# Expert blocks of 168 slots instead of 192, and gathers that leave out padded slots, in a fused decoder-layer kernel

## The reference, cut to what matters

```python
scores = jax.nn.sigmoid((x @ lp['router_w']).astype(jnp.float32))
_, idx = lax.top_k(scores + lp['router_bias'].astype(jnp.float32), TOP_K)      # 8 of 64 experts
gate = jnp.take_along_axis(scores, idx, axis=-1)
gate = gate / jnp.sum(gate, axis=-1, keepdims=True) * ROUTED_SCALE
...
def swiglu(x, w_gate, w_up, w_down):
    return (jax.nn.silu(x @ w_gate) * (x @ w_up)) @ w_down
...
routed = jax.ops.segment_sum(y, tok, num_segments=N)      # y: each expert's rows, times gate
return routed + swiglu(x, lp['w_sh_gate'], lp['w_sh_up'], lp['w_sh_down'])
```

## Time and profile before

| | |
|---|---|
| median of three runs | 2907.5 us |
| profiled execution, device time | 2899.51 us |
| its span, first to last instruction | 2896.6 us |
| mean granted TensorE clock in it | 0.954 |
| first `gate` matmul of the first expert block (L1955) | at 1755.67 us |
| first `gate` matmul of the last, 64th, block | at 2813.67 us |
| PE busy, of the span | 2581.3 us (89%) |
| DVE busy | 1356.9 us (47%) |
| ACT busy | 1054.3 us (36%) |
| POOL busy | 595.0 us (21%) |

### The profile page before, as it was taken

How to read it: one execution, slowest core, us unless ns; L and a number is a source line. 1 busy time by engine, 2 the same in 40 slices (tenths; PEclk the granted TensorE clock), 3 DMA queues, 4 the chain that set the end, 5 groups by cost and what they waited for, 6 DMA issues and landing times. The chain is left out here.

```text
span 2896.6 us, 38101 instructions
## 1 busy us (share of the span) xinstructions
PE 2581.3 (89%) x13546; PEld 1943.9 (67%) x13546; DVE 1356.9 (47%) x2762; ACT 1054.3 (36%) x1687; POOL 595.0 (21%) x421
## 2 busy tenths in 40 slices
PE   7879997989996659999999697999999999999990
PEld 5447775656445555666645346898998898998990
DVE  0423334520007640100146425777777777777774
ACT  1133333320002210000012005666666676766762
POOL 1010002200000000000004402344343443443433
PEclk9989998999999979999999798999999999999995
DMA  4000003321001014111013118999999999999974
GB/s 123 0 15 0 0 0 148 146 84 37 0 0 40 0 35 130 29 37 43 0 57 100 45 73 288 273 292 277 284 290 281 283 287 274 289 283 286 283 192 149
DMA packets 151712, 395.12 MB, mean 136 GB/s; under 512 B 43318, under 2 KB 87430, under 8 KB 125014
## 3 DMA queue, kind: packets, MB, share of 16 engines
q1 hardware_dynamic: 116166, 269.90, 27.7%
q0 software_dynamic: 35488, 124.43, 17.7%
HBM read 325.74 MB, written 69.13 MB: 136 GB/s over the span
## 5 line engine op out<-in xcount | busy, mean ns | idle before, releaser
L1958 PE MATMUL banks<-split 128*128 128x384 f32 x1792 | 538.6, 363 | 0.0
L2072 DVE TENSOR_TENSOR split<-rest,split 128x2048 fp32r<-128x2048 f32 x192 | 438.8, 2285 | 108.7 <-ACT split L2016 108.7
L1956 PE MATMUL banks<-split 128*128 128x192 f32 x2048 | 482.9, 256 | 0.0
L1978 PE MATMUL banks<-split 128*128 128x512 f32 x1536 | 406.5, 407 | 22.9 <-ACT rest L2029 18.8
L1956 PEld LDWEIGHTS banks<-split 128*128 128x128 f32 x2048 | 389.3, 192 | 2.7
L2016 ACT CAST split<-rest 128x2048 fp32r<-128x2048 f32 x192 | 359.3, 1904 | 66.0 <-DMA rest<-in_w_exp_gate 61.0
L1408 PE MATMUL banks<-big 128*128 128x368 f32 x1152 | 358.6, 474 | 15.2 <-DMA big<-in_w_br_hg 15.2
L1906 POOL DMA_INDIRECT y_rows<-rest x128 | 271.3, 2119 | 335.3 <-ACT rest L2029 298.5
L1958 PEld LDWEIGHTS banks<-split 128*128 128x128 f32 x1792 | 339.1, 189 | 0.0
L1978 PEld LDWEIGHTS banks<-split 128*128 128x128 f32 x1536 | 276.4, 190 | 78.3 <-ACT rest L2029 23.0
L1408 PEld LDWEIGHTS banks<-big 128*128 128x128 f32 x1152 | 219.9, 191 | 153.5 <-issue 17.3
(11 more groups left out here) (331 smaller groups left out, 3343.6 us busy)
## 6 DMA issues: line engine op xcount, KB each, us to landing
rest<-in_w_exp_gate SPq DMA_DIRECT2D x64, 1024.0 KB, 9.7
rest<-in_w_exp_up SPq DMA_DIRECT2D x64, 1024.0 KB, 6.0
rest<-in_w_exp_down SPq DMA_DIRECT2D x64, 1024.0 KB, 7.2
big<-in_w_in SPq DMA_DIRECT2D x27, 512.0 KB, 4.1
big<-in_x_prompt SPq DMA_DIRECT2D x14, 512.0 KB, 5.9
x_rows<-big SPq DMA_DIRECT2D x9, 512.0 KB
y_rows<-big SPq DMA_DIRECT2D x9, 512.0 KB, 2.6
big<-in_w_in SPq DMA_DIRECT2D x1, 4096.0 KB, 15.4
```

What stands on the lines that cost most here:

```text
L1956: ins = pe.matmul(PS[:, banks[f], 0:CAP], wr[:, s, j, LO, at:at + 128], x[:, k, 0:2], start=False, stop=False)
L1958: ins = pe.matmul(PS[:, banks[f], 0:2 * CAP], wr[:, s, j, HI, at:at + 128], x[:, k], start=False, stop=(k == KD - 1))
L1978: ins = pe.matmul(PS[:, DBANK[c]], hr[:, a, f, HALF * hf:HALF * hf + 128], wr[:, s, DOWN, b, at:at + 512], start=(f == 0 and j == 0), stop ...
L2072: dve.tensor_tensor(wr[:, s, j, LO], raw[:, s, j], wr[:, s, j, HI].bitcast(F32), ALU.subtract).then_inc(parted[j], 1)
```

## The change

CAP goes from 192 to 168, and with it every size that is made from it: HALF from 96 to 84, VCAP from 1152 (6 * 192) to 1176 (7 * 168), KOVER from 5 to 6, the table's slots from 73920 to 75432. The rows behind T are written no more and `x1_rows` ends at T. The gathers are given `bounds_check=T - 1, oob_is_err=False`: an entry whose row number is over T - 1 is to be left out, and the row of the buffer stays as it is. So that nothing undefined stands there at first, POOL fills the gather buffer with zeros once, ahead of its first gather, and waits for that.

```diff
-CAP = 192
+CAP = 168
 HALF = CAP // 2
 VCAP = -(-T // CAP) * CAP
...
-        sp.dma_start(S.x1_dram[T:T + 128], S.x1[:, 0]).then_inc(x1_out, 16)
-        sp.dma_start(S.x1_dram[T + 128:T + CAP], S.x1[0:CAP - 128, 1]).then_inc(x1_out, 16)
-        sp.wait_ge(x1_out, 16 * (NT + 2))
+        sp.wait_ge(x1_out, 16 * NT)
...
-    passed = sem("e_passed")
+    passed, xg_zero = sem("e_passed"), sem("e_xz")
...
                 pool.indirect_dma_start(out=xg[0:HALF, s, hf], out_offset=None, in_=S.x1_dram,
-                                        in_offset=bass.IndirectOffsetOnAxis(ap=gi[0:HALF, s, 2 * hf:2 * hf + 1].bitcast(I32), axis=0)
-                                        ).then_inc(xg_in[s], 16)
+                                        in_offset=bass.IndirectOffsetOnAxis(ap=gi[0:HALF, s, 2 * hf:2 * hf + 1].bitcast(I32), axis=0),
+                                        bounds_check=T - 1, oob_is_err=False).then_inc(xg_in[s], 16)
...
         for s in range(2):
             pool.sem_inc(si_free[s], 1)
+        pool.memset(xg.rearrange("p a b c -> p (a b c)")[0:HALF], 0.0).then_inc(xg_zero, 1)
+        pool.wait_ge(xg_zero, 1)
         gather(0, 0)
         gather(1, 0)
...
-        S.x1_dram = nc.dram_tensor("x1_rows", [T + CAP, DM], F32).ap()
+        S.x1_dram = nc.dram_tensor("x1_rows", [T, DM], F32).ap()
```

## The result

| | before | after |
|---|---|---|
| median of 11 runs each, same chip | 2911.65 us | 2921.63 us |
| lowest to highest | 2904.23 to 2917.02 | 2911.84 to 2930.65 |
| ratio, with 95% interval | | 1.0035 [1.0021, 1.0049] |
| profiled execution, its own time | 2899.51 us | 2921.63 us |
| its span | 2896.6 us | 2919.4 us |

The forecast was 2897 us and faster; the measured time is inside the range, on the other side of no change. The two profiled executions differ by more (22.8 us of span) than the medians do (10.0 us), because the stages ahead of the expert blocks also took longer in the second: the expert stage's first instruction is at 1740.47 us in the trace of before and at 1750.89 us in that of after. So I compare the expert stage alone, from there to the first instruction of the next stage (2842.05 and 2865.36 us): 1101.6 us before, 1114.5 after, +12.9 us.

The account below looks back on a forecast made before the run. PE was taken to bound the expert blocks, with DMA nearly full. The loop's 15.8 us plus 0.15 for the late entries gave 15.95 per block: -9.5 us, last block -0.8, together -10.3, so 2897 us; range 2874 to 2926.

Parts of the forecast that it names:

- Two more blocks: Expert blocks: 66 instead of 64, each a full one; at 16.62 us each that alone is +33.2 us.
- PE's floor: PE's own work per expert block: from 16.21 to 15.40 us, through shorter wide matmuls and transposes.
- DMA relief: DMA engines in the expert blocks: 82 rows less per block at 287 ns a row, 1.5 us of 15.8 less.
- The loop: From one odd block's scatter through the next gather to the next odd scatter: 32.70 us to 31.6 per two blocks.
- The sign that was named: In the expert blocks, PE's transposes would wait for the gather in every second block.
- The late entries: ACT's wait for table entries requested behind the `down` matrix: 0.15 us per block left of the 0.41 excess.
- Ends: First and last expert block: 3.5 us fill and first period 1.3 us shorter, together nothing; last block 0.8 us shorter.
- The slower rival: Expert blocks: the loop does not shrink and gathers get dearer, 16.4 us per block, +19 us, 2926 us; chance 0.21.
- threshold of 32.4 us: Length of the loop over which, in the slower rival, 66 blocks cost more than 64 did.

Follow-up runs that it names:

- cap_168: The kernel before with blocks of 168 slots in place of 192, gathers without a bounds check; ratio to before 1.0066.
- skip_192: The kernel after with blocks of 192 slots in place of 168, padded rows still left out of gathers; ratio to before 0.9975.
- ent_168: The kernel after with the table entries requested ahead of the `down` matrix; ratio to before 0.9938.
- gat_168: The kernel after with the next even block's gather issued ahead of the wait for the odd block's scatter to land; ratio to before 0.9927.
- skip_184: The kernel after with blocks of 184 slots in place of 168, so halves of 92 rows; ratio to before 1.1446.
- both_168: The kernel after with table entries requested ahead of `down` and the gather ahead of the wait for the scatter; ratio to before 0.9844.
- both_192: The kernel before with table entries requested ahead of `down` and the gather ahead of the wait for the scatter; ratio to before 0.9918.
- gat_192: The kernel before with the next even block's gather issued ahead of the wait for the odd block's scatter; ratio to before 0.9959.

## Why the prediction failed

- **Two more blocks.** Right: 66, all of full length.
- **PE's floor.** Right: forecast 15.40 us, measured 15.35. The narrow matmul stayed at 0.11 us. The wide one lost the 0.02 us that the forecast gave it (0.179 to 0.156 us, medians). The Trainium skill's rule in "TensorE: Matmul & The Clock Gate", section LDWEIGHTS, is columns / 1.2 ns, an estimate of 107 ns for 128 columns, and the row of the narrow one agrees with it.
- **DMA relief.** The rows were as counted, their price not. q0 took 16 x 800 x 0.371 = 4749 us for 14,976 rows, 317 ns each where the earlier trace rows gave 287. Per block that is 96.6 us of engine time in place of 109.9: 0.8 us of relief on each of 16 engines, not 1.5. The small packets are little of it, 92 us in all (56 before). A packet of 4 KB itself took 311 ns on average where it took 284 before; it took 300 in cap_168 and in skip_192. Why is open.
- **The loop.** Right: forecast 31.6 us for two blocks, one is 31.41 in the trace. Forecast for the loop as the only wait: 15.8 us per block; ent_168, which has that wait alone, takes 15.72, so 31.44 for two. The sign that was named, a wait of the transposes for the gather in every second block, came in part: 17 times in 32 pairs. There is luck in the size: the forecast was the middle of two bounds, and the relief that it leaned on was half of what it assumed.
- **"The late entries remain, but a block that they stretch gives the next gather time, so the two don't add up: of the 0.41 us I leave 0.15."** This is the step that failed. The loop alone cost 0.37 us (ent_168), near the 0.40 of the forecast, and both waits 0.93 (after), so that the entries on top of the loop were 0.56 where 0.15 was left for them. Alone they cost 0.60 in the trace of gat_168, and some 0.37 by the median of its runs. Two errors lie in the step. I took the cost of the entries at its old size. Their way hardly changed: ACT's first part in even blocks begins 12.64 us after the block's start before (median) and 12.70 after. But in blocks without a wait it began at 12.20 us before and at 11.40 after: the deadline came 0.8 us nearer with PE's floor, and the waits went from 57.0 us in 19 to 72.1 us in 20. The same thing that I had worked out for the loop, a fixed way against a shorter block, I did not work out for the entries. And I argued, without a row, that a block which the entries stretch would give the gather time. It gives little: odd blocks, which hold the gather's wait, take 15.90 us after and 16.02 in ent_168, 0.06 us per block on average, while even ones take 16.66 after and 15.42 in ent_168. With 0.56 in the place of 0.15 and the measured floor and loop the sum is 15.35 + 0.37 + 0.56 = 16.28 us, 64 x 16.28 = 1042 against 1030, the +11.4 us of the trace; since 0.56 is itself the difference of after and ent_168, this locates the miss and doesn't test it.
- **Ends.** The fill took 3.51 us as forecast, and the first gather came 4.56 us after the stage's first instruction in place of 3.22. The first period is 0.7 us longer where I had it 1.3 shorter, and its rate fell from 364 to 351 GB/s. Little can be read from that: over all runs the first period was 24.2 to 30.5 us, one execution each. The last block, which I had 0.8 us shorter, was 0.4 longer, from its first matmul to the next stage.
- **The slower rival.** Its sum, 16.4 us per block, came near to 16.28, with half of its reason. The packet counts fit 84 rows on 14 engines, and the gather's instruction on POOL takes 1042 ns (median) where it took 943; half of that is the bounds check, for in cap_168 it takes 992. But the loop did shrink, and both waits are as large in cap_168, which has no bounds check. What it priced by the loop alone is for the larger part the entries. And its threshold of 32.4 us was too high: 64 blocks of 16.10 us already take the 1030.3 us of before, so that with 0.15 for the entries a loop of over 31.9 us was enough for slower. The forecast of 31.6 was 0.3 us away from it.

Of the 12.9 us that the stage became longer, 11.4 are the middle periods, 0.7 the first one, 0.4 the stretch ahead of it and 0.4 the last block. The part ahead of the stage, 10.4 us, is in code that the change doesn't touch but for two writes less in routing and a longer slot table. Medians put the whole difference at 10.0 us.

## What to carry to other kernels

When an edit makes the bounding engine faster, list every transfer that lands close to its deadline, and move each deadline by the gain. A latency that cost 0.17 us per block at a block of 16.2 us cost 0.60 at 15.4 in the traces (0.24 and 0.37 by the medians). Before shrinking a tile, look at what is issued ahead of the small transfers (1.5 KB behind 1 MB here) and at what a gather is queued behind: two reorderings without any less work gave 0.8% here, and 1.6% together with the smaller tile that alone had cost 0.66%. And choose row counts of indirect transfers so that 16 divides them, or test them at the size meant: 92 rows cost 6.6 us per block with the old orders, 84 rows nothing with the new ones.

## What the runs showed of the hardware

- **The row count of an indirect transfer matters, not only its size.** By the packet counts the rows on the fullest engine are 6, 6, 5, 8 and 23 for 96, 84, 80, 88 and 92 rows. 92 rows made a block 6.6 us longer than 96 did, with the DMA engines busy 0.67 of the time.
- **A long wait costs clock too.** PE's granted clock was 0.86 in the middle periods of skip_184, in which PE was idle for 363 of 1429 us; the others have 0.98 to 1.00. In the middle periods of both_168, with no idle time, it never left the upper level; in after 17.1 of 1041.7 us were at the lower.
- **A left-out row is a packet all the same,** a small one. It moves no 4 KB, and the bounds check makes the gather's instruction on POOL longer, not shorter: 992 to 1042 ns with 84 rows (cap_168, after), 943 to 1094 ns with 96 (before, skip_192; medians).
- **A DMA share of 0.97 to 1.00 was not a bound.** both_192 and both_168 have shares of 1.00 and 0.97 and no wait of PE; gat_192 has 0.98 and little; skip_184 has the lowest share and the longest waits. The share tells of the work, the waits tell of the order.
- **Narrow matmuls.** With a load of 128 columns of weights each, 160, 168 and 192 columns take the same 0.11 us (medians 0.109, 0.109 and 0.108), while 320, 336 and 384 take 0.150, 0.156 and 0.179.
- **Untouched stages vary.** The last instruction of attention ended at 617.8 us in the profile of before and at 625.8 in that of after. Sums against a single execution have to be made stage by stage. And one profile can be an outlier of its kernel: the four executions of gat_168 lie 22.9 us apart, those of both_168, which has no waits left, 1.4.
